# K and V projected in the first MLP's stage, and one attention stage by groups of heads, with scores on half arrays

## The reference

```python
q, k, v = qkv_proj(h, w_qkv, b_qkv, pos)       # 16 query heads, 4 key/value heads of 64; rotary on the first 16 of 64
mask = (kpos <= qpos) & (kpos >= qpos - WINDOW) & (kpos >= 0)
scores = where(mask, einsum(q, k) * 64 ** -0.5, -inf)
m = max(max(scores), sink)
probs = exp(scores - m) / (sum(exp(scores - m)) + exp(sink - m))
o = einsum(probs, v)                            # samples: 128 cached keys and the new one
xp = xp + mp[2] * (o @ w_o)
hp = pre_norm(xp, norm2_g[i], mp[3], mp[4])
xp = xp + mp[5] * (square(relu(hp @ w_up)) @ w_down)
```

## Time and profile before

| | us |
|---|---|
| median of 3 runs (lowest to highest) | 3216.46 (3216.35 to 3218.57) |
| the profiled execution's own time | 3221.39 |
| its span in the trace | 3219.6 |
| PE busy in the span | 2790.9 |
| DVE, ACT, POOL busy | 1344.6, 932.4, 673.1 |
| mean granted clock of PE | 0.929 |

### The profile page before, as it was taken

The page is one execution under the profiler, slowest core; times in us unless marked ns, Lnnn a source line. Parts: engine busy times, 40 slices in busy tenths (PEclk is TensorE's granted clock), DMA queues, the critical chain, the costliest instruction groups (busy, mean ns, idle before and its releaser), DMA issues. The chain is left out here.

```text
span 3219.6 us, 48197 instructions
## 1 busy us (share of the span) xinstructions
PE 2790.9 (87%) x19702; PEld 2608.4 (81%) x19702; DVE 1344.6 (42%) x2484; ACT 932.4 (29%) x1792; POOL 673.1 (21%) x459
## 2 busy tenths in 40 slices
PE   5497878948883999999999987977779999999998
PEld 2357768947772889999999987966578999999998
DVE  3354676328884742121221253627736212122223
ACT  2354624312212442120211331115534202121121
POOL 0011111113334111222122303322220222222230
PEclk8698989979996899999999998968989999999999
DMA  5665758665545512222222202120020111111121
GB/s 229 230 253 181 231 176 251 212 165 113 100 92 169 169 47 86 86 79 85 86 86 84 75 1 66 52 58 1 0 66 14 53 47 46 46 47 52 47 66 53
DMA packets 375526, 321.98 MB, mean 100 GB/s; under 512 B 118006, under 2 KB 345018, under 8 KB 368268
## 3 DMA queue, kind: packets, MB, share of 16 engines
q1 hardware_dynamic: 352412, 274.43, 28.5%
q0 software_dynamic: 8256, 28.48, 2.5%
q10 hardware_dynamic: 14672, 16.39, 1.8%
HBM read 246.79 MB, written 74.56 MB: 100 GB/s over the span
## 5 line engine op out<-in xcount | busy, mean ns | idle before, releaser
L791 POOL TENSOR_TENSOR t_wL<-t_raw,t_wH 128x1024 fp32r<-128x1024 f32 x116 | 278.6, 2402 | 1206.1 <-ACT t_wH L906 1206.1
L810 PE MATMUL t_acc<-twoH,t_wH 128*128 128x344 f32 x1392 | 449.2, 323 | 6.8 <-DVE twoL L1110 4.5
L810 PE MATMUL t_acc<-oneH,t_wH 128*128 128x344 f32 x1392 | 449.6, 323 | 5.8 <-DVE oneL L1110 4.3
L811 PE MATMUL t_acc<-oneL,t_wH 128*128 128x344 f32 x1392 | 445.8, 320 | 0.0
L811 PE MATMUL t_acc<-twoL,t_wH 128*128 128x344 f32 x1392 | 445.8, 320 | 0.0
L812 PE MATMUL t_acc<-twoH,t_wL 128*128 128x344 f32 x1392 | 445.7, 320 | 0.0
L812 PE MATMUL t_acc<-oneH,t_wL 128*128 128x344 f32 x1392 | 445.6, 320 | 0.0
L1060 DVE SCALAR_TENSOR_TENSOR X<-t_acc,mod,X 128x344 f32<-128x344 f32 (+1 forms) x240 | 137.5, 573 | 631.0 <-PE t_acc L812 627.4
L1130 DVE TENSOR_TENSOR t_g<-t_g 128x344 f32<-128x344 f32 x192 | 99.3, 517 | 554.6 <-ACT t_g L926 554.6
L810 PEld LDWEIGHTS t_acc<-twoH,t_wH 128*128 128x128 f32 x1392 | 262.2, 188 | 20.2 <-issue 11.2
L810 PEld LDWEIGHTS t_acc<-oneH,t_wH 128*128 128x128 f32 x1392 | 262.3, 188 | 19.2 <-issue 10.1
(11 more groups left out here) (459 smaller groups left out, 5524.0 us busy)
## 6 DMA issues: line engine op xcount, KB each, us to landing
t_raw<-in_mlp_down SPq DMA_DIRECT2D x64, 512.0 KB, 4.0
t_raw<-in_mlp_up SPq DMA_DIRECT2D x62, 512.0 KB, 4.0
ada_ring<-in_ada_w SPq DMA_DIRECT2D x24, 1024.0 KB, 6.8
t_shared<-in_ada_w SPq DMA_DIRECT2D x24, 1024.0 KB, 6.3
kvrb_hx<-hx_saved ACTq DMA_DIRECT2D x16, 516.5 KB, 3.9
kvr_work<-scr_L SPq DMA_DIRECT2D x16, 516.0 KB, 4.6
q_wraw<-in_at_wqkv SPq DMA_DIRECT2D x12, 512.0 KB, 3.8
scr_Yc<-c_Yt ACTq DMA_DIRECT2D x10, 512.0 KB, 3.2
```

Source lines behind the costliest of these rows:

```text
L791: pool.tensor_tensor(low, raw[:, w % 2], high.bitcast(F32), ALU.subtract).then_inc(s_low, 1)
L810: pe.matmul(out, high[:, k, :], h[:, k, third[t]], start=(k == 0), stop=False)
L811: pe.matmul(out, high[:, k, :], l[:, k, third[t]], start=False, stop=False)
```

## The change

- Layer 0's tail gets 12 more units at its end, "kv": 4 panels by 3 thirds, V's as panels 0 and 1, K's as 2 and 3. They use the norm's output third by third (in the last third K comes first). Two more panels, the first two of Q, are only loaded and split there. X is saved to `x_saved` in thirds, and the K/V results are written over blocks 0 to 3 of X. The last third's `mean_square`, `roots` and `normed` are placed between the kv units.
- `Panels`, `stage_qkv`, `stage_attend_samples` and `stage_attend` go. One stage, `stage_attention`, has the remaining Q panels, the samples and the prompt. It goes by groups of heads: group k needs Q's panels 2k and 2k+1 alone and runs over all 8 tiles. Six of Q's 24 units come ahead of the first step, two are in step 0, and the rest are put singly in the steps (`units_before`).
- The rotary partners are fetched by four DMAs a panel within SBUF (`partner`), and DVE combines them in three operations over all 1032 columns (`rope`). `Kd` is made by eight DMAs.
- A head's scores are two products of 64 rows, one on either half of the array. No zeroed query buffer and no copy of V is needed. The sink is a 257th column of `S`, so the maximum with changed sign and the sum of exponentials include it.
- On PE the order in a step is `values(n - 1)`, `turn(n)`, `scores(n + 2)`. The values' heads are now two on one half of the columns, then two on the other.
- The samples' transposes and scores stand in the last group's first four steps, their softmax in later steps, their 16 products with the cached values at the end.
- The attention's output goes to X in full float32. Layer 1's tail splits it with `prepare`, as layer 0's does, and loads the saved X back in thirds. Its first two weight panels are loaded in the attention stage.

```diff
@@ unit_order
+    if layer == 0:
+        order += [("kv", p, t) for t in range(NT) for p in ((0, 1, 2, 3) if t < NT - 1 else (2, 3, 0, 1))]
@@ stage_tail, SyncE
+            def save(t):
+                sp.wait_ge(s_add, added[at_unit["d", LAST + DB - 1, t]])
+                sp.dma_start(net.x_saved[:, :, third[t]], X[:, :, third[t]]).then_inc(s_saved[t], 16)
...
                 weights(w)
+                if layer == 1 and w in (5, 9, 11):
+                    t = (5, 9, 11).index(w)
+                    sp.wait_ge(s_pl, (t + 1) * DB)
+                    load_x(t)
+                if panels[w] in (("kv", 1), ("kv", 3)):
+                    save(panels[w][1] // 2)
...
-            if layer == 1:
+            if layer == 0:
+                save(2)
@@ stage_tail, TensorE
+                if order[u] == ("kv", 1, 0):
+                    mean_square(1, NT - 1)
                 u += 1
-            if layer == 0:
-                mean_square(1, NT - 1)
@@ stage_tail, ScalarE
+            def key_or_value(u):
...
+                act.wait_ge(s_done, u + 1)
+                act.wait_ge(s_saved[t], 16)
+                act.wait_ge(s_xn, (NT + t + 1) * DB)
+                act.activation(X[:, p, third[t]], acc[u % 4][:, 0:TT], ACT.Identity, bias=net.param[:, at:at + 1]).then_inc(s_kv, 1)
+
             if layer == 0:
                 affine(0)
-                high(0)
-                high(1)
-                for b in range(DB):
-                    prepare(0, b)
-                    if b in (1, 3, 5, 7):
-                        high(2 + b // 2)
-            else:
-                for w in range(DB):
-                    high(w)
+            high(0)
+            high(1)
+            for b in range(DB):
+                prepare(0, b)
+                if b in (1, 3, 5, 7):
+                    high(2 + b // 2)
...
+                if kind == "kv":
+                    key_or_value(u)
+                    j = u - at_unit["kv", 0, 0]
+                    if j == 1:
+                        roots(1, NT - 1)
+                    if 2 <= j < 6:
+                        normed(1, NT - 1, 2 * j - 4)
+                        normed(1, NT - 1, 2 * j - 3)
@@ stage_attention
+        def units_before(n):
+            if n == 0:
+                return (6, 7)
+            k, t = group(n)
+            if t == TILES - 1 and k < LAST - 1:
+                return (6 * k + 12,)
+            return (6 * k + 7 + t,) if k < LAST and t <= 4 else ()
...
+            def partner(j):
+                x, y = roped(j), part[:, j % 2, :]
+                if j >= 2:
+                    sp.wait_ge(s_q, 3 * (j - 1))
+                    sp.wait_ge(s_rot, j - 1)
+                for h in range(2):
+                    for a in range(2):
+                        to, of = 64 * h + 8 * a, 64 * h + 8 - 8 * a
+                        sp.dma_start(y[to:to + 8], x[of:of + 8]).then_inc(s_part[j % 2], 16)
...
+            sp.wait_ge(s_zero, 1)
+            partner(0)
+            partner(1)
+            for i in range(2):
+                sp.dma_start(cs[:, i, :], io["const_wide"][:, (1 + i) * TOK:(2 + i) * TOK]).then_inc(s_cs, 16)
+            weights(2)
+            weights(3)
+            sp.dma_start(mask[:], io["const_mask"]).then_inc(s_in, 16)
+            sp.dma_start(sinks[:], io["at_sink"].to_broadcast([128, HEADS])).then_inc(s_in, 16)
+            for i in range(2):
+                sp.wait_ge(s_rot, i + 1)
+                for h in range(2):
+                    for a in range(2):
+                        sp.dma_start(Kd[64 * a:64 * a + 64, 2 * i + h, :], X[64 * h:64 * h + 64, 2 + i, :]).then_inc(s_kd, 16)
+            partner(2)
...
+            def scores(n):
...
+                for j in range(2):
+                    for a in range(2):
+                        r = slice(64 * a, 64 * a + 64)
+                        ins = pe.matmul(pS[n % 2][:, 2 * a + j, lo:256], Q[r, (2 * k + j) % 4, t * 128:t * 128 + 128], Kd[r, k, first:first + 256 - lo],
+                                        start=True, stop=True, skip_group_check=True, tile_position=(64 * a, 0))
...
+            for u in range(6):
+                unit(u)
+                if u == 3:
+                    k_rows()
+            scores(0)
+            scores(1)
+            for n in range(STEPS):
+                k, t = group(n)
+                two = (2 * t, 2 * t + 1) if k == LAST and t < 4 else None
+                for u in units_before(n):
+                    unit(u)
+                if two:
+                    turn_cache(two[0])
+                if n:
+                    values(n - 1)
+                turn(n)
+                if two:
+                    sample_scores(two[0])
+                    turn_cache(two[1])
+                if n + 2 < STEPS:
+                    scores(n + 2)
+                if two:
+                    sample_scores(two[1])
...
+            def evict(u):
...
+                act.activation(Q[:, p % 4, third[t]], bank[:, 0:TT], ACT.Identity, bias=net.param[:, at + p:at + p + 1]).then_inc(s_q, 1)
+                if t == NT - 1 and p + 2 < DB:
+                    high(p + 2)
...
+            def rope(j):
+                x, y = roped(j), part[:, j % 2, :]
+                dve.wait_ge(s_part[j % 2], 64 * (j // 2 + 1))
+                dve.wait_ge(s_cs, 32)
+                dve.tensor_tensor(y, y, cs[:, 1, :], ALU.mult).then_inc(s_r, 1)
+                dve.tensor_tensor(x, x, cs[:, 0, :], ALU.mult).then_inc(s_r, 1)
+                dve.wait_ge(s_r, 2 * j + 2)
+                dve.tensor_tensor(x, x, y, ALU.add).then_inc(s_rot, 1)
...
+            dve.wait_ge(s_in, 32)
+            for j in range(4):
+                rope(j)
+            dve.wait_ge(s_qz, 1)
+            queries(0)
+            masked(0)
+            for n in range(STEPS):
+                k, t = group(n)
+                if n + 1 < STEPS:
+                    masked(n + 1)
+                normal(n)
+                if k < LAST and t in (2, 5):
+                    rope(2 * k + 4 + t // 5)
+                if k < LAST and t == 5:
+                    queries(k + 1)
```

More of the change, by code:

```diff
@@ L193, in build @@
                 net.HH, net.HL = one
-                attention(net)
+                with stage(net):
+                    stage_attention(net)
             with ExitStack() as pair:
@@ new lines, in stage_attention @@
+        banks = [acc[:], flat(pS[0])[:, 0:512], flat(pS[0])[:, 512:1024]]
+        tb = [pT[:, 2 * i:2 * i + 2].rearrange("p g j c -> p (g j) c") for i in range(2)]
+        rows = flat(pS[1])
+        s_raw, s_high, s_low, s_done, s_q = [sem("raw0"), sem("raw1")], sem("high"), sem("low"), sem("done"), sem("q")
+        s_part, s_cs, s_in, s_kd, s_zero, s_r, s_rot = [sem("part0"), sem("part1")], sem("cs"), sem("in"), sem("kd"), sem("zero"), sem("r"), sem("rot")
+        s_tv, s_tvev, s_vt, s_vtev, s_krow, s_kev, s_out, s_ks, s_vs = sem("tv"), sem("tvev"), sem("vt"), sem("vtev"), sem("krow"), sem("kev"), sem("out"), sem("ks"), sem("vs")
@@ new lines, in values @@
+            def values(n):
+                k, t = group(n)
+                blocks = 1 if t == 0 else 2
+                pe.wait_ge(s_pt, n + 1)
+                if n >= 1:
+                    pe.wait_ge(s_x, n)
+                else:
+                    pe.wait_ge(s_vtev, 2)
+                for g in range(4):
+                    a, i = g // 2, g % 2
+                    for j in range(blocks):
+                        ins = pe.matmul(pO[64 * a:64 * a + 64, i, :], Vt[:, t - blocks + 1 + j, k * HD:(k + 1) * HD], PT[:, g, j, :], start=(j == 0), stop=(j == blocks - 1), skip_group_check=True, tile_position=(0, 64 * a))
+                ins.then_inc(s_o, 1)
```

903 lines of the change are left out of this document (360 added, 543 removed).

## The result

The changed kernel takes 3136.14 us (median of 4 runs, 3130.81 to 3138.42) against 3217.15 (4 runs, 3216.35 to 3218.57) for the kernel before beside it: a ratio of 0.9745, with a 95% interval of 0.9728 to 0.9762. The forecast was 3122 in a range of 3098 to 3158. The profiled execution took 3138.42 with a span of 3136.4, where the one before had 3219.6: 83.2 us less, against 95 in the working.

The account below looks back on a forecast made before the run. PE, busy 87% of the span, was taken as the bound. Terms 47 + 50 + 230 + 12 = 339 against 441.4 give -102, second tail +7, so -95: 3126 profiled, 3122 us for runs; range 3098 to 3158.

Parts of the forecast that it names:

- The K/V units cover the norm: End of the first MLP: the last third's norm runs under 12 K/V units; the attention stage starts 47 us after the MLP.
- T: Reference time: the end of the first MLP's last unit, 1917.5 us in the profile of the kernel before.
- the second tail: Layer 1's tail after attention: splitting X and waiting for weight panels delays PE's first unit, ending 20 to 21; +7 us.
- the first term: Start of the second tail: blocks wait behind weight panels and POOL, so PE's first unit ends at 20 to 21; +7 us.
- Loads of X at nothing: Second tail: X's loads (10.1 us) come before add 1 is four banks late, so they cost nothing.
- The start, 56.5 for 50: Attention stage's start: the first transposes of probabilities come 50 us in, after PE idles for a rotation.
- so all is there near 15: Attention stage's start: SP's loads, through mask and sinks (2.1 MB), have landed near 15 us into the stage.
- Rotation late: Rival: partner transfers take 4 us more, start costs 8 more, six later rotations stall DVE 1 to 2 each; 3140; chance 0.13.
- The steps, 221.4 for 230: Attention's 31 steps after the first: 7.3 us with a unit, 6.2 to 6.3 without; together 230 us.
- the samples' 6.2 and the clock's 7.5: Last group's steps: 6.2 us for the samples' products and softmax, 7.5 for PE's lower clock without units.
- The switch of tiling at nothing: Attention steps on PE: changes between full array, row halves and column halves get no time in the step sums.
- Slower than before: Rival: PE's clock sits at 1.2 GHz throughout the merged attention stage; 3317 us; chance 0.03.

Follow-up runs that it names:

- e4: Changed kernel with the last third's norm held back behind the eighth K/V unit instead of the second; 3145.9 us, ratio 0.9769 to the kernel before.
- e3: Changed kernel with scores over all 128 rows of the array instead of two row halves; 3145.7 us, ratio 0.9773 to the kernel before.
- e1: Changed kernel with scores(n + 2) ahead of turn(n) on PE instead of behind it; 3113.2 us, ratio 0.9669 to the kernel before.
- e7: Changed kernel with the last stage's second and third thirds of X both prepared during the first third's units; 3122.9 us, ratio 0.9696 to the kernel before.
- e6: Changed kernel with ACT preparing all eight first-third blocks before high(2) to high(5) in the last stage; 3132.0 us, ratio 0.9724 to the kernel before.
- e9: Changed kernel with scores first, values alternating, units 6 and 7 first, cos/sin first, first third prepared first, last third prepared early; 3081.2 us, ratio 0.9574.
- e8: Changed kernel with cos and sin loaded before K's partner rows, and DVE's mask/sinks wait behind K's rotations; 3121.9 us, ratio 0.9700 to the kernel before.
- e2: Changed kernel with values of the four heads in order 0, 2, 1, 3, alternating column halves; 3133.4 us, ratio 0.9732 to the kernel before.

## Why the prediction was right, and by how much it missed

**Right in its mechanisms.** The K/V units cover the norm (47.6 us for 47, last block at T+26.7 for T+26, and e4 prices the cover at 14.0). Four scores on two halves of 64 rows take 1.14 for the 1.1 taken, and e3 shows that it is the halves that do it. PE is the bound with a unit and DVE's chain without, which e1 shows by taking the scores out of that chain. What idles PE ahead of turn(0) is a rotation that waits for its partner rows.

**The term that was mis-sized: the second tail, +7 by the prediction, +18.7 by the trace.** What the prediction priced came as priced: the first unit ended at 20.4 us (20 to 21), and PE is 7.2 us behind the kernel before from its second unit on. The waits that make this are partly others: ACT waited for four panels in a row, 4.72, 1.65, 1.89 and 1.59 us, ahead of blocks, not only ahead of blocks 6 and 7, and DVE's lows were held by POOL for whole operations (below). What the prediction left out is the stretch behind it. Each unit of the second third carries a block of the last third for ACT and DVE, which the kernel before had from its attention stage, and DVE has them beside the adds and the norm of the third before. DVE's last six lows of these blocks start 4.9 us apart (from 2319.63 to 2343.97), two of them held by POOL, and a unit takes 3.8. So PE runs out of blocks near 2345, and the waits with the slow clock behind them cost 10.1 us. e7 takes this away. The last 1 us or so comes late in the stage and was not looked into. e6 shows that the first term could be had back too, though not in full. With both, e9's rest is 12.4 less.

**Loads of X at nothing.** In the changed kernel they cost PE nothing, as forecast: DVE waits 5 us for the first (above) and 5.8 us in all for the other two, and at none of these places does PE wait. That they delay the blocks near 2345 a little is not excluded. With the first unit earlier it is no longer nothing: in e9 the first add still waits for X at 2235.92, and PE, out of banks, for this add, 1.78 us at 2236.60.

**The start, 56.5 for 50.** The step that failed is "so all is there near 15", and what hangs on it. SP's queue needed 12 us only to issue its loads (the mask alone 4.24, where the sinks take 0.43), the sinks landed 3.4 us later, and K's rows delayed the copies into a_Kd, which hold SP for 7.22 us ahead of the queries' partner rows. The last rotation, forecast to end at 39, ended at 43.6, which is 4.6 of the 6.5; from there to turn(0) it took 12.9 where the forecast has 11. e8 takes 10.0 of the start away without a transfer less. "Rotation late" was the rival with the right place, at four fifths of its 8 us at the start, and its six stalls in the steps didn't come: the steps with a rotation and a unit take 7.55, like the one without.

**The steps, 221.4 for 230.** Thirteen long steps with a unit took 100.6 (96.7 forecast): eleven at 7.57, and two of 8.7 that follow PE's longest waits for DVE (4.04 us ahead of the first) and run at a clock of 0.80. The values' 0.43 is in all of them; the prediction bounded it by 0.7 and took 0. The three short ones took 18.6 (19.2), those with a rotation and queries 23.5 (24.9). The twelve without a unit were to take 89.3 with the samples and the slow clock, and took 78.7. Three of these are plain at 6.1 (6.2 to 6.3 forecast). The nine of the last group took 60.4, where nine at 6.3, the samples' 6.2 and the clock's 7.5 make 70.4. In order they are 4.60, 5.55, 8.17, 9.36, 7.74, 6.91, 6.91, 6.14 and 5.02. So 3.7 of the 10 us is that three of them, beside the group's first tile and at the very end, have less to do and were priced as full steps. The other six are 7.4 over 6.3 each, where samples and clock together were priced at 13.7. The samples' products (they stand in the third to the sixth) and the low clock (0.50 in the fourth, 1.00 in the sixth) fall partly into the same steps and partly into waits that these steps have anyway, PE being busy 47 of the 60 us; which of the two prices was too high these rows don't say. That this error offsets the start's is luck.

**The switch of tiling at nothing.** The prediction read one place, where transposes at the low clock begin as the values end, and took no price. e1 and e3 give 0.1 to 0.2 us for a change. In one step that is little; over the 31 steps, with one change too many in the order of the code, e1 gains some 2.6 us of its 18.2 by it (0.19 on eleven steps with a unit, 0.14 to 0.20 on the three short ones).

**Slower than before** did not come near: the steps had a clock of 0.92, and the low clock was confined to the start, the two steps of 8.7 and the last group. e2 shows that the mechanism exists all the same: there the last nine steps ran at 0.57.

What stays open is the code ahead of T: identical in all these kernels, it ended up to 9 us apart from one profile to another, and 3.6 us of the miss is this. Nothing was tried for its cause. Why e2's last group ran at the low clock and e9's did not is open too. PE's busy share in the eight steps before that group is no answer: 54.1 of 59.0 us in the changed kernel, 52.2 of 58.0 in e2, and 48.6 of 55.3 in e9, the lowest of the three, which keeps its clock.

## What to carry to other kernels

When work is merged under a bound engine, price the order in which each queue issues: six edits of order alone, without a product or a transfer less, gave some 50 us more by the stretches of the traces (55 by the medians), on top of the 81 that the change gave. Where small products stand in a chain with waits, shorten the chain first: the clock that came back was worth more than the chain itself here (8.5 of 11.5 us in e1's last nine steps). And a stage that takes over preparation from the one before needs its own look at the engines that prepare, not only at its first product.

## What the runs showed of the hardware

**DVE held by POOL for the whole operation.** The timeline of the changed kernel, POOL's split of a weight panel and DVE's low half that starts under it; the same operation alone is above it in time:

```profile
2334.12 0.52 DVE L1059 TENSOR_TENSOR oneL<-X,oneH 128x344 fp32r<-128x344 f32 x1 [1.23 <-ACT oneH L880]
2338.26 2.35 POOL L706 TENSOR_TENSOR wL<-raw,wH 128x1024 fp32r<-128x1024 f32 x1 [7.50 <-ACT wH L825]
2338.59 2.40 DVE L1059 TENSOR_TENSOR oneL<-X,oneH 128x344 fp32r<-128x344 f32 x1 [2.18 <-ACT oneH L880]
```

DVE's 0.52 us become 2.40, and it ends 0.38 after POOL's operation does. So it is not slowed in part: nearly all of its work comes after POOL's end. The prediction took a mean (0.51 to 0.75), which hides this. The Trainium skill's "SBUF — State Buffer" ("SBUF: two separate sides") has it as an exclusive lock, held for the whole instruction, between a GpSimd operation that reads SBUF and a VectorE operation with two SBUF inputs; the trace agrees, with these numbers.

**Which half of the array comes next.** Sixteen products on column halves take 1.14 us when heads alternate between the halves and 1.58 when two heads of one half precede two of the other, at the same clock and for the same products.

**A change of tiling** costs PE 0.17 us at full clock by e1 and 0.14 by e3 (0.28 for two), worked out from differences between kernels; it is visible only from start to start, not in a record's length.
